# An RWKV-7 mixer's decay sums moved from the next pair's inversion levels into a pair's tail

## The reference

```
w_log = -softplus(-(w0 + tanh(zw) @ w2)) - 0.5
decay = exp(-exp(w_log))
def step(S, inp):
    r_t, w_t, k_t, v_t, a_t, b_t = inp
    sa = einsum("dbhij,dbhj->dbhi", S, a_t)
    S = S * w_t[..., None, :] + sa[..., :, None] * b_t[..., None, :] + v_t[..., :, None] * k_t[..., None, :]
    return S, einsum("dbhij,dbhj->dbhi", S, r_t)
```

## Time and profile before

| | |
|---|---|
| median of 3 runs | 3207.24 us (3206.11 to 3211.26) |
| the profiled execution's own time | 3217.23 us |
| its span | 3215.4 us |
| TensorE busy | 3085.9 us, 96% |
| VectorE busy | 2070.4 us, 64% |
| ScalarE busy | 1659.3 us, 52% |
| GpSimd busy | 612.5 us, 19% |

### The profile page before, as it was taken

How to read it: one execution, slowest core, us unless ns; L and a number is a source line. 1 busy time by engine, 2 the same in 40 slices (tenths; PEclk the granted TensorE clock), 3 DMA queues, 4 the chain that set the end, 5 groups by cost and what they waited for, 6 DMA issues and landing times.

```text
span 3215.4 us, 56503 instructions
## 1 busy us (share of the span) xinstructions
PE 3085.9 (96%) x20863; PEld 2655.4 (83%) x20863; DVE 2070.4 (64%) x3472; ACT 1659.3 (52%) x2673; POOL 612.5 (19%) x517
## 2 busy tenths in 40 slices
PE   8999988989999999999999998889899999999998
PEld 7899877777888888888788997777788888888886
DVE  5775555676777777445568655566767777764554
ACT  5555554446555555445455565444465555544444
POOL 2000453440212222000000014334402221220000
PEclk9999998999999999999999999899899999999999
DMA  6666101114656666666556650011256565656654
GB/s 205 179 179 188 46 2 52 62 59 137 190 183 196 187 185 200 218 194 193 158 170 192 189 170 2 2 65 53 65 174 189 182 189 183 189 193 214 192 186 151
DMA packets 265227, 479.22 MB, mean 149 GB/s; under 512 B 17314, under 2 KB 81148, under 8 KB 264380
## 3 DMA queue, kind: packets, MB, share of 16 engines
q1 hardware_dynamic: 265020, 476.48, 48.2%
HBM read 474.32 MB, written 2.10 MB: 148 GB/s over the span
## 4 chain that ended last, share of the span: by engine, by line
PE 88%; DVE 6%; ACT 3%; issue 1%; DVEq 1%; ACTq 0%; POOL 0%; SPq 0%; DMA 0%; POOLq 0%
PE ps L637 87%; PE ps L641 1%; ACT L1263 1%; DVE wlo L1770 1%; DVE TN L1829 0%; DVE upair L1783 0%; DVE XS L1820 0%; ACT UA L1263 0%; DVE H L1802 0%; DVE AR L2174 0%; DVE TN L2195 0%; ACT XS L1263 0%; DVE rf L2209 0%; POOL H L574 0%; ACT whi L1263 0%
## 5 line engine op out<-in xcount | busy, mean ns | idle before, releaser
L1770 DVE TENSOR_TENSOR wlo<-ring,whi 128x1024 fp32r<-128x1024 f32 (+4 forms) x905 | 1086.7, 1217 | 692.5 <-ACT whi L1263 686.1
L637 PE MATMUL ps<-upair,whi 128*128 128x512 f32 x4032 | 1416.2, 396 | 6.2 <-DVE upair L1783 5.3
L1263 ACT ACTIVATE whi<-ring 128x1024 fp32r<-128x1024 f32 (+4 forms) x947 | 941.0, 1002 | 803.1 <-PE ps L637 763.5
L637 PE MATMUL ps<-upair,wlo 128*128 128x256 f32 x4032 | 1131.3, 281 | 0.0
L637 PEld LDWEIGHTS ps<-upair,whi 128*128 128x128 f32 x4032 | 757.3, 188 | 185.5 <-issue 5.9
L637 PEld LDWEIGHTS ps<-upair,wlo 128*128 128x128 f32 x4032 | 762.9, 189 | 0.3 <-issue 0.2
L637 PE MATMUL ps<-whi,upair 128*128 128x390 f32 (+2 forms) x1280 | 367.4, 364 | 0.0
L619 POOL TENSOR_TENSOR YB<-YB 128x1024 f32<-128x1024 f32 x22 | 125.3, 5694 | 837.7 <-DVE YB L1793 837.7
L637 PE MATMUL ps<-whi,ghi 128*128 128x512 f32 x704 | 274.4, 390 | 0.0
L637 PE MATMUL ps<-whi,glo 128*128 128x512 f32 x704 | 274.0, 389 | 0.0
L637 PE MATMUL ps<-wlo,ghi 128*128 128x512 f32 x704 | 273.9, 389 | 0.0
(11 more groups left out here) (310 smaller groups left out, 3725.5 us busy)
## 6 DMA issues: line engine op xcount, KB each, us to landing
ring<-in_w_up_dram SPq DMA_DIRECT2D x352, 512.0 KB, 3.8
ring<-in_w_down_dram SPq DMA_DIRECT2D x176, 512.0 KB, 4.3
ring<-in_w_in_dram SPq DMA_DIRECT2D x128, 384.0 KB, 3.5
ring<-in_w_out_dram SPq DMA_DIRECT2D x64, 512.0 KB, 3.7
ring<-in_w_ple_gate_dram SPq DMA_DIRECT2D x64, 512.0 KB, 4.3
ring<-in_w_in_dram SPq DMA_DIRECT2D x51, 512.0 KB, 4.5
ring<-in_w_in_dram SPq DMA_DIRECT2D x64, 390.0 KB, 3.4
ring<-in_w_in_dram SPq DMA_DIRECT2D x32, 396.0 KB, 3.5
```

The lines of the kernel that those rows point to most:

```text
L637: return pe.matmul(o_, a, b, start=start, stop=stop, skip_group_check=True)
L1263: return act.activation(o_, i_, f, **kw)
L1770: v.tensor_tensor(wlo[:, slot % RING, :, 0:w], ring[:, slot % RING, :, 0:w], whi[:, slot % RING, :, 0:w].bitcast(F32), SUB).then_inc(S["lo ...
```

## The change

On VectorE, the decay sums of pair c + 1 are no longer made after levels 0 and 1 of pair c. The pair c = 0 still makes those of pair 1 there. Those of pair c + 2 are made in the tail of pair c, behind the state scaling and in front of `rw_coefficients(c + 1)` and `rw_start`, each direction after a wait for `rw_ops` of pair c + 1, because GpSimd's products of that pair still read `sums`. On ScalarE, the exponentials of both directions are issued after levels 2 and 3 instead of 3 and 4, in all pairs with a next one.

```diff
                         if more and lv == 2:
                             rw_norms(c + 1, n + 1, False, True)
-                        if more and lv in (3, 4):
-                            rw_decays(c + 1, n2 + 2, lv - 3)
+                        if more and lv in (2, 3):
+                            rw_decays(c + 1, n2 + 2, lv - 2)
                         if not more:
                             gate_factors(lv)
...
                     def between_levels(lv):
                         if c and lv == 0:
                             rw_variance(n - 1)
-                        if more and lv in (0, 1):
-                            rw_decays(c + 1, lv)
+                        if c == 0 and lv in (0, 1):
+                            rw_decays(1, lv)
...
+                    if c + 2 < RC:
+                        for d in range(2):
+                            v.wait_ge(S["rw_ops"], n2 + (3 + d))
+                            rw_decays(c + 2, d)
                     if more:
                         rw_coefficients(c + 1, n + 1)
                         rw_start(v.snap(n2 + 2))
```

## The result

The changed kernel takes 3241.86 us (3241.43 to 3242.16, 4 runs) against 3208.18 us before (3206.11 to 3211.26, 4 runs): ratio 1.0096, 95% interval 1.0078 to 1.0115. It is slower by 25 to 37 us. The forecast was 3209.8 us, in a range of 3201.5 to 3217.5.

What follows compares the result with a forecast made beforehand. TensorE, with 88% of the chain of waits, was taken to bound the kernel. The terms -7.92 + 11.76 - 1.56 + 0.3 = +2.6 us on the median 3207.24 gave 3209.8 us, range 3201.5 to 3217.5.

Steps and rivals of the forecast that it cites:

- Part 1: Level 1, second and third pairs of each layer: moving the decay sums removes 1.98 us in each of four, -7.92 us.
- Part 2: Level 4, six pairs: earlier exponentials delay ScalarE's copy by 1.96 us each, +11.76 us; 1.56 us come back after level 4.
- Level 5's last copy: ScalarE in six pairs: with no exponentials left there, the copy comes 0.29 us earlier, 0.26 showing, 1.56 us gained in all.
- Part 3: Tails of each layer's first two pairs: the sums mostly fit the 5.1 us of room, +0.3 us, bounds 0 and 4.7.
- rw_start's slack: Tail: rw_start's last transpose ends 1.35 us before the x product that reads it, part of the 5.1 us of room.
- the higher price: Tail: by the skill's letter each group of sums waits out a whole GpSimd operation, costing the upper bound instead of 0.3 us.
- The exchange of stalls: Inversion levels: the level 1 stall is exchanged for one of 2.54 us in level 4, +2.6 us in the whole sum.
- The clock: TensorE behind stalls: a low stretch costs 1.60 us; nothing in the sum, bounds -6.4 and +6.4 us.
- The bound on the other side: TensorE's clock: if the new level 4 stalls draw no low stretch, four stretches go, -4 x 1.60 = -6.4 us.
- Rival B: Level 4 stalls draw the lower clock in each pair: 2.6 + 4 x 1.60 = +9.0 us, 3216.2 us, chance 0.20.

Runs made afterwards that it cites:

- e1: Changed kernel with the exponentials back behind levels 3 and 4, only the sums moved; 3195.05 us against 3215.12 before, ratio 0.9944.
- the filled stall: Changed kernel with ten more pairs of filler products on TensorE in the level 4 stall of six pairs; 3216.92 us, ratio 0.9999 to before.
- e10_last_filled: Kernel with sums and exponentials in the tails, plus 28 pairs of filler products in each layer's last pair, level 3; 3199.90 us, ratio 0.9966 to before.
- filler series: Changed kernel with three, six or ten extra pairs of filler products in the level 4 stall; 3239.65, 3233.85 and 3216.92 us.

## Why the prediction was wrong

- **Part 1, sums out of the first levels: right.** t is 1.21 us behind x in 1.1; four stalls of 1.98 us went. Alone it gains (ratio 0.9944), more than the stalls and with short low stretches gone besides.
- **Part 2, exponentials: the mechanism and its 1.96 us were right.** The stall is 2.48 us, 2.54 forecast, and the copy is 1.93 us later. Level 5's last copy waits for TensorE alone, as forecast.
- **Part 3, the tail: right.** 0.6 us in a tail under rw_out (e1), 0 in the changed kernel; the sums lengthen to 6.3 us there, just above the 5.4 to 6.1 I gave, and rw_start's slack takes most of it. By the Trainium skill (SBUF — State Buffer, Who interferes with whom) a VectorE instruction with two SBUF inputs contends with a GpSimd instruction that reads SBUF, and the lock is exclusive. In e1 the scans, which have two SBUF inputs, took 0.94 us beside rw_out instead of 0.42, and agree; but the higher price that I worked out beside it wasn't paid, because the slack behind took it.
- **The exchange of stalls: right, as far as 8 us can tell.** With TensorE kept busy in them, the changed kernel is at 0.9999 of before.
- **The clock: the step that failed.** I took 1.60 us for a low stretch from the level 1 stall of 2.1, and bounded the whole by four stretches more than before, +6.4 us. In the sum it stood at nothing. It measured 4.05 to 5.54 us, in all six pairs: 29.9 us. With that the same sum is 2.6 + 29.9 = 32.5 us, where 33.7 was measured. That they lie so close is partly luck: the sum leaves out the last pairs (4.0 us against the filled stall) on one side and, on the other, the short stretches that the profile of before has and the changed kernel mostly hasn't. In the profiles the pairs differ by 24.75 us only. The bound on the other side was wrong too: of the four stretches behind level 1 stalls that -4 x 1.60 takes away, two stand behind the stalls of 1.0 and 2.0, which stay. Rival B named the mechanism and was given 3216.2 and a chance of 0.20; its price of a stretch was too low by a factor of about three, and it let only four of them come on top.
- **What I could have read.** The trace of before has a longer stall than those of level 1 in the last pairs, in level 3 of pair 1.3, and behind it a stretch at 0.53 of 9.8 us, not 3.5. That is the row of before shown with `e10_last_filled`. It is inside the inversion, with products on 64 rows around it, as level 4 is. The level 1 stalls are followed by keys and norms on 128 rows. I priced a stall in one place by the stretch behind a stall in another. It would have been a better price, not a sure one: the same stall drew some 20 us in the changed kernel.

What decides how long the clock stays low is not settled. The filler series shows that TensorE's idle time in that place bears on whether it falls, but equal idle times went both ways. That 2.04 us in level 1 drew some 3 us, or nothing in 1.1 and 1.2, and 1.95 us in level 4 drew 11 us suggests that the place matters as well; no run moved a stall of one length from place to place.

## What to carry to other kernels

An edit that exchanges one TensorE stall for another of the same length isn't neutral: ask of each stall what clock follows it, take the price from a stretch behind a stall of that length in the same kind of work, and give it a wide range. When an engine's step must be moved, look for the place where that engine idles and nobody waits (the tail, here for both engines), and try each half of a two-part edit alone: one half gained 0.6%, the other lost 1.3%. Filler products in a stall that can't be removed are a cheap test, and sometimes a cheap cure, but measure the whole: the low clock may just move on.

## What the runs showed of the hardware that was not expected

- Behind 2.48 us of idle on TensorE stood 12.8 us at 1.2 GHz, during which it was busy 12.74 us: the higher clock did not come back while it was busy with the products of this place.
- Twenty products of 64 rows by 256 columns, 1.26 us, at the start of the stall kept the clock up in all six pairs; twelve did in two pairs of six, and six in none, though in one the low stretch was short.
- The last pair of layer 1, with the same stall of 4.57 us in both kernels, had 9.8 us at the lower level before and some 20 us in the changed kernel.
- The changed kernel's runs agree to 0.02% (3241.4 to 3242.2), those of before spread over 0.2% (4 runs) in the same comparison and over 0.5 to 0.9% (17 to 20 runs) in the others.
